# Gates and ups with both halves of h in one 512-column product, added at the evacuation

## The reference, cut to what matters

```python
proj = jnp.einsum("bsd,dn->bsn", h, w_in)
q, k, v, f_logit, g_b, g_c, hc, gate_conv, gate_attn = jnp.split(proj, _SPLITS, axis=-1)
...
merged = jax.nn.sigmoid(gate_conv) * ya_d + jax.nn.sigmoid(gate_attn) * yb_d
...
gu = jnp.einsum("bsd,df->bsf", h, w_gate_up)
g, u = jnp.split(gu, 2, axis=-1)
return jnp.einsum("bsf,fd->bsd", jax.nn.silu(g) * u, w_down)
```

## Time and profile before

| | |
|---|---|
| median of 3 runs | 1022.47 us |
| the profiled execution | 1022.51 us |
| its span, first to last instruction | 1021.0 us |
| time around the span | 1.5 us |
| instructions | 16052 |
| mean granted TensorE clock | 0.995 |
| HBM read | 223.54 MB |

### The profile page before, as it was taken

The page is one execution under the profiler, slowest core; times in us unless marked ns, Lnnn a source line. Parts: engine busy times, 40 slices in busy tenths (PEclk is TensorE's granted clock), DMA queues, the critical chain, the costliest instruction groups (busy, mean ns, idle before and its releaser), DMA issues.

```text
span 1021.0 us, 16052 instructions
## 1 busy us (share of the span) xinstructions
PE 995.3 (97%) x6874; PEld 914.1 (90%) x6874; DVE 688.0 (67%) x986; ACT 491.4 (48%) x688; POOL 33.3 (3%) x51
## 2 busy tenths in 40 slices
PE   7999999899999999999999999999999899999997
PEld 6988899789898998899889999997997689999996
DVE  5766756769757768887778768667676766545443
ACT  5644544454334345555564334455667664434341
POOL 3000000010000000100000000001000010000000
PEclk9999999999999999999999999999999999999999
DMA  9663367556897775786467778875643257555511
GB/s 366 262 229 101 126 251 280 206 188 246 314 259 289 296 278 193 265 313 247 166 248 266 300 280 308 312 293 179 214 137 125 83 130 262 171 201 171 201 42 41
DMA packets 33303, 225.65 MB, mean 221 GB/s; under 512 B 3997, under 2 KB 4277, under 8 KB 6864
## 3 DMA queue, kind: packets, MB, share of 16 engines
q1 hardware_dynamic: 31104, 219.00, 59.8%
q0 software_dynamic: 1552, 4.88, 1.4%
q10 hardware_dynamic: 576, 0.74, 0.2%
HBM read 223.54 MB, written 1.08 MB: 220 GB/s over the span
## 4 chain that ended last, share of the span: by engine, by line
PE 88%; DVE 6%; ACT 3%; issue 1%; DMA 1%; POOL 0%; ACTq 0%; DVEq 0%
PE psum L569 18%; PE psum L571 18%; PE psum L570 18%; PE psum L595 8%; PE psum L596 8%; PE psum L597 8%; DVE low L496 2%; PE psum L814 2%; ACT high L490 1%; PE psum L659 1%; PE psum L660 1%; PE psum L661 1%; PE psum L311 1%; PE psum L880 1%; DMA x_res<-in_x 1%
## 5 line engine op out<-in xcount | busy, mean ns | idle before, releaser
L496 DVE TENSOR_TENSOR low<-raw,high 128x2048 fp32r<-128x2048 f32 (+1 forms) x160 | 362.3, 2276 | 162.7 <-ACT high L490 162.1
L569 PE MATMUL psum<-h_hi,high 128*128 128x256 f32 x1504 | 428.6, 285 | 0.0
L571 PE MATMUL psum<-h_hi,low 128*128 128x256 f32 x1504 | 425.5, 283 | 0.0
L570 PE MATMUL psum<-h_lo,high 128*128 128x256 f32 x1504 | 425.5, 283 | 0.0
L490 ACT ACTIVATE high<-raw 128x2048 fp32r<-128x2048 f32 (+1 forms) x160 | 301.0, 1899 | 53.1 <-DMA raw<-in_gate_up 27.9
L569 PEld LDWEIGHTS psum<-h_hi,high 128*128 128x128 f32 x1504 | 288.4, 192 | 5.2 <-issue 2.3
L570 PEld LDWEIGHTS psum<-h_lo,high 128*128 128x128 f32 x1504 | 288.5, 192 | 1.1
L571 PEld LDWEIGHTS psum<-h_hi,low 128*128 128x128 f32 x1504 | 288.5, 192 | 0.0
L595 PE MATMUL psum<-high,y_hi 128*128 128x512 f32 x328 | 129.1, 394 | 2.9 <-DVE y_lo L902 1.7
L596 PE MATMUL psum<-low,y_hi 128*128 128x512 f32 x328 | 128.0, 390 | 0.0
L597 PE MATMUL psum<-high,y_lo 128*128 128x512 f32 x328 | 127.7, 389 | 0.0
(11 more groups left out here) (173 smaller groups left out, 904.7 us busy)
## 6 DMA issues: line engine op xcount, KB each, us to landing
raw<-in_gate_up SPq DMA_DIRECT2D x66, 1024.0 KB, 5.1
raw<-in_ada SPq DMA_DIRECT2D x48, 1024.0 KB, 6.4
raw<-in_down SPq DMA_DIRECT2D x33, 1024.0 KB, 5.3
raw<-in_mix SPq DMA_DIRECT2D x14, 1024.0 KB, 5.1
raw<-in_moba_qk SPq DMA_DIRECT2D x8, 1024.0 KB, 7.2
raw<-in_diff_qk SPq DMA_DIRECT2D x8, 1024.0 KB, 6.2
raw<-in_qk SPq DMA_DIRECT2D x4, 1024.0 KB, 14.7
raw<-in_branch SPq DMA_DIRECT2D x4, 1024.0 KB, 6.1
```

The lines of the kernel that those rows point to most:

```text
L496: nc.vector.tensor_tensor(low[i % N_RAW][:, s], raw[i % N_RAW][:, s], high[n % N_HI][:, s].bitcast(F32), ALU.subtract).then_inc(*rest.up(key))
L569: nc.tensor.matmul(to, a, hi(k), start=first, stop=False)
L570: nc.tensor.matmul(to, a, lo(k), start=False, stop=False)
L571: m = nc.tensor.matmul(to, r, hi(k), start=False, stop=last and j > j0)
```

## The change

h_hi and h_lo become the two halves of one tile, so that for a given k they lie side by side as 512 columns. A new `pe_both` takes the place of `pe_still` for the eight mixer gates and for gates and ups of groups 1 to 10 of each feed-forward part (68 slabs: 8 and 60). For each k and column block it issues two matmuls in place of three: the weights' high half with both halves of h (512 columns), and the weights' low half with h_hi (256 columns, onto the first 256). A column block now fills a whole bank, so a product takes two neighbouring banks, the first of them even. The sum over the two halves is made at the evacuation: ACT copies the second halves to SBUF (`act_low`), DVE adds the first halves out of PSUM (`dve_low`, in place), and only then come Silu or Sigmoid (ACT, now from SBUF) and gate times up (DVE, now from SBUF). A product's banks are free when `dve_low` has run (`joined`). The transposes of probabilities 6 and 7 in the first attention get banks 4 and 5 by number.

```diff
--- before.py
+++ after.py
@@ -177,8 +177,8 @@
         low = [sb(f"low{i}", [P, SLAB], F32R) for i in range(N_RAW)]
         high = [sb(f"high{i}", [P, SLAB], F32R) for i in range(N_HI)]
         x_res = sb("x_res", [P, NT, D])
-        h_hi = sb("h_hi", [P, KC, S], F32R)
-        h_lo = sb("h_lo", [P, KC, S], F32R)
+        h_both = sb("h_both", [P, KC, 2, S], F32R)
+        h_hi, h_lo = h_both[:, :, 0, :], h_both[:, :, 1, :]
         y_hi = sb("y_hi", [P, KC, S], F32R)
         y_lo = sb("y_lo", [P, KC, S], F32R)
         work = sb("work", [P, 2 * NT * D])
@@ -209,7 +209,8 @@
         ident_r = sb("ident_r", [H, H], F32R)
         diff_stat = sb("diff_stat", [P, NT * H])
         minus_half = sb("minus_half", [P, NT * H])
-        psum = [ctx.enter_context(nc.psum_tensor(f"psum{i}", [P, 512], F32)) for i in range(8)]
+        psum_two = [ctx.enter_context(nc.psum_tensor(f"psum{i}", [P, 2, 512], F32)) for i in range(4)]
+        psum = [psum_two[i // 2][:, i % 2, :] for i in range(8)]
         gain_dram = nc.dram_tensor("gain_dram", (4, D), F32, kind="Internal").ap()
         bias_dram = nc.dram_tensor("bias_dram", (H, BIAS_W), F32, kind="Internal").ap()
 
@@ -285,6 +286,29 @@
             owner[at] = list(freed)
             bank_of[key] = at
             return psum[at]
+
+        def two_banks(key, *freed):
+
+            turn[0] += turn[0] % 2
+            yield from bank(key, *freed)
+            yield from bank((key, "second"), *freed)
+            return psum_two[bank_of[key] // 2]
+
+        def halves(key):
+
+            o = psum_two[bank_of[key] // 2]
+            return o[:, :, 0:S], o[:, :, S:2 * S]
+
+        def act_low(key, place, *free):
+
+            yield from act.wait_ge(slab, key)
+            for signal, done in free:
+                yield from act.wait_ge(signal, done)
+            nc.scalar.activation(place, halves(key)[1], ACT.Copy).then_inc(*evacuated.up(("low", *key)))
+
+        def dve_low(key, place):
+            yield from dve.wait_ge(evacuated, ("low", *key))
+            nc.vector.tensor_tensor(place, halves(key)[0], place, ALU.add).then_inc(*joined.up(key))
 
 
         def columns_of(stage):
@@ -569,6 +593,22 @@
                         nc.tensor.matmul(to, a, hi(k), start=first, stop=False)
                         nc.tensor.matmul(to, a, lo(k), start=False, stop=False)
                         m = nc.tensor.matmul(to, r, hi(k), start=False, stop=last and j > j0)
+            m.then_inc(*slab.up(n, (name, index), *alias))
+
+        def pe_both(name, index, ready, freed, alias=()):
+
+            n = NUM[name, index]
+            yield from pe.wait_ge(rest, n)
+            wh = high[n % N_HI][:, :].rearrange("p (k n) -> p k n", k=KC)
+            wl = low[SLOT[n]][:, :].rearrange("p (k n) -> p k n", k=KC)
+            o = yield from two_banks((name, index), freed)
+            for k in range(KC):
+                for signal, key in ready(k):
+                    yield from pe.wait_ge(signal, key)
+                for j in range(2):
+                    a, r = wh[:, k, j * P:(j + 1) * P], wl[:, k, j * P:(j + 1) * P]
+                    nc.tensor.matmul(o[:, j, :], a, h_both[:, k, :, :], start=k == 0, stop=False)
+                    m = nc.tensor.matmul(o[:, j, 0:S], r, h_hi[:, k, :], start=False, stop=k == KC - 1)
             m.then_inc(*slab.up(n, (name, index), *alias))
 
         def pe_moving(name, parts, data, ready, kcs, k_all, freed, tag, between={}):
@@ -695,11 +735,11 @@
             yield from pe_turn(before, 1)
             yield from pe_rows(f, 1)
             for g in range(1, FG):
-                yield from pe_still(gate_up, base * 2 * FG + g, h_of, h_ready(before), [[(evacuated, ("silu", f, g))]])
+                yield from pe_both(gate_up, base * 2 * FG + g, h_ready(before), (joined, (gate_up, base * 2 * FG + g)))
                 if g == 1:
                     yield from pe_turn_rows(f)
-                yield from pe_still(gate_up, base * 2 * FG + FG + g, h_of, h_ready(before), [[(produced, ("hidden", f, g))]],
-                                    [("up", f)] if g == FG - 1 else [])
+                yield from pe_both(gate_up, base * 2 * FG + FG + g, h_ready(before), (joined, (gate_up, base * 2 * FG + FG + g)),
+                                   [("up", f)] if g == FG - 1 else [])
                 if g < FG - 2:
                     yield from pe_down(f, g - 1)
                 if g in meanwhile:
@@ -715,11 +755,13 @@
             for g in range(1, FG):
                 gate, up = (gate_up, base * 2 * FG + g), (gate_up, base * 2 * FG + FG + g)
                 yield from act_next(*gate)
-                yield from act.wait_ge(slab, gate)
-                nc.scalar.activation(ffn_tmp(g)[:, 0], pair(bank_of[*gate, 0]), ACT.Silu).then_inc(*evacuated.up(("silu", f, g)))
+                yield from act_low(gate, ffn_tmp(g)[:, 0])
+                yield from act.wait_ge(joined, gate)
+                nc.scalar.activation(ffn_tmp(g)[:, 0], ffn_tmp(g)[:, 0], ACT.Silu).then_inc(*evacuated.up(("silu", f, g)))
                 if g == 1:
                     yield from act_turn_rows(f)
                 yield from act_next(*up, AHEAD if g < FG - 1 else FAR)
+                yield from act_low(up, ffn_tmp(g)[:, 1])
                 yield from act.wait_ge(produced, ("hidden", f, g))
                 if g >= 4:
                     yield from act.wait_ge(slab, NUM[down, base * FG + g - 4])
@@ -737,12 +779,14 @@
             for g in range(1, FG):
                 gate, up = (gate_up, base * 2 * FG + g), (gate_up, base * 2 * FG + FG + g)
                 yield from dve_next(*gate)
+                yield from dve_low(gate, ffn_tmp(g)[:, 0])
                 if g == 1:
                     yield from dve_turn_rows(f)
                 yield from dve_next(*up, AHEAD if g < FG - 1 else FAR)
+                yield from dve_low(up, ffn_tmp(g)[:, 1])
                 yield from dve.wait_ge(evacuated, ("silu", f, g))
-                yield from dve.wait_ge(slab, up)
-                nc.vector.tensor_tensor(ffn_tmp(g)[:, 1], pair(bank_of[*up, 0]), ffn_tmp(g)[:, 0], ALU.mult).then_inc(
+                yield from dve.wait_ge(joined, up)
+                nc.vector.tensor_tensor(ffn_tmp(g)[:, 1], ffn_tmp(g)[:, 1], ffn_tmp(g)[:, 0], ALU.mult).then_inc(
                     *produced.up(("hidden", f, g)))
                 yield from dve.wait_ge(hi_made, ("hidden", f, g))
                 s = slice(2 * (g % 4), 2 * (g % 4) + 2)
@@ -872,9 +916,9 @@
                                                    op0=ALU.mult, op1=ALU.add)
             m.then_inc(*weighted.up((tag, h)))
 
-        def pe_turn_probs(tag, h):
+        def pe_turn_probs(tag, h, at=None):
             z = prob[probs_of(tag, h)[0]]
-            o = yield from bank(("turn", tag, h), (probs_copied, (tag, h)))
+            o = yield from bank(("turn", tag, h), (probs_copied, (tag, h)), at=at)
             yield from pe.wait_ge(weighted, (tag, h))
             for c in range(3):
                 m = nc.tensor.transpose(o[:, c * P:(c + 1) * P], z[:, c * P:(c + 1) * P], ident)
@@ -919,7 +963,7 @@
                 nc.tensor.matmul(o[rows, 0:S], v(0), p[:, 0:S], start=True, stop=False)
                 nc.tensor.matmul(o[rows, P:S], v(1), p[:, S:3 * P], start=False, stop=True).then_inc(*applied.up(("s1", h)))
             if 0 <= n - 2 < H:
-                yield from pe_turn_probs("s1", n - 2)
+                yield from pe_turn_probs("s1", n - 2, n - 4 if n >= H else None)
             if n < H:
                 h = n
                 part = slice((h % 2) * HD1, (h % 2 + 1) * HD1)
@@ -1130,7 +1174,7 @@
                 yield from pe_attend1(6 + g)
             for n in range(2):
                 for g in range(4):
-                    yield from pe_still("mix", 6 + 4 * n + g, h_of, ready, [[(evacuated, ("gate", n, g))]])
+                    yield from pe_both("mix", 6 + 4 * n + g, ready, (joined, ("mix", 6 + 4 * n + g)))
                     if n == 0 and g < 3:
                         yield from pe_attend1(H + g)
             conv_of = (lambda k: y_hi[:, AC + k, :], lambda k: y_lo[:, AC + k, :])
@@ -1257,10 +1301,11 @@
                 for g in range(4):
                     index = 6 + 4 * n + g
                     yield from act_next("mix", index)
-                    yield from act.wait_ge(slab, ("mix", index))
+                    two = slice(2 * g, 2 * g + 2)
                     yield from act.wait_ge(lo_made, ("conv", 1))
-                    nc.scalar.activation(place[:, 2 * g:2 * g + 2, :], pair(bank_of["mix", index, 0]), ACT.Sigmoid).then_inc(
-                        *evacuated.up(("gate", n, g)))
+                    yield from act_low(("mix", index), place[:, two, :])
+                    yield from act.wait_ge(joined, ("mix", index))
+                    nc.scalar.activation(place[:, two, :], place[:, two, :], ACT.Sigmoid).then_inc(*evacuated.up(("gate", n, g)))
                     if n == 0 and g < 3:
```

(6 more changed lines are left out.)

## The result

The changed kernel takes 1042.03 us (median of 4 runs, 1038.28 to 1043.22), the kernel before 1023.19 us in the same comparison (1021.98 to 1024.10). The ratio is 1.0175, 95% interval 1.0156 to 1.0193: slower by 19 us. The profiled execution took 1043.22 us with a span of 1041.7 us, 20.7 us more than the span before. The direction was forecast, the size was not: 1031.4 us was predicted, and 1042 lies above the range of 1016 to 1039.

The account below looks back on a forecast made before the run. The prediction took PE, busy 97% of the span, as the bound. From 1022.5 us it took 11.8 saved, 17.3 lost to waits and 3.4 to the clock, giving 1031.4 us, range 1016 to 1039.

Parts of the forecast that it names:

- saving of the pairs: PE matmuls of all 68 slabs: two matmuls per set instead of three save 11.9 ns a set, 12.9 us in all.
- the six slabs ahead of a wait: Gate 1 three times, up 5, up 10 twice: their saving is void, 1.1 us, leaving 11.8 saved.
- up 1 waits for gate 1's banks: Up 1 in feed-forward parts 0, 1, 2 waits for DVE's addition: 3.8, 5.1 and 1.5 us, together 10.4.
- gate 6 waits for the flips' copies: Part 0: four flip products take banks 0 to 3, so gate 6 waits for DVE's copies, 3.4 us late.
- down 10 waits for the last y_lo: Ends of parts 0 and 1: the last hidden group's added copy and additions delay down 10 by 1.4 and 2.1 us.
- the clock: PE's granted clock falls behind two of five new gaps: 3.4 us, between 0 for none and 8.6 for all.
- (a): Rival at up 1 and the flips: additions come early, up 1 waits about 1 us, 1016.5 us; chance 0.11.
- (d): Rival: DVE's loop becomes the bound where ada slabs are dense, 9 us more, 1040 us; chance 0.08.
- (b): Rival: up 1's stalls let other engines get ahead; flips and ends cost nothing, clock stays; 1021.1 us; chance 0.11.
- (c): Rival on PE's pairs: no fixed cost goes away, 2.5 ns saved a set instead of 11.9; 1041.6 us; chance 0.05.

Follow-up runs that it names:

- the first experiment: Changed kernel with the transposes of group 0 given bank 4 by number; 1028.58 us against 1024.49 for the kernel before, ratio 1.0040.
- The filled wait: Changed kernel with 17, 23 and 6 small unused fp32 matmuls on PE ahead of up 1; 1036.05 us against 1024.49 for the kernel before.
- the grouped form: Changed kernel with all 16 matmuls of 512 columns issued before the 16 of 256 in each product; 1035.80 us, kernel before 1024.49.
- the version with the other two edits: Changed kernel with bank 4 for group 0's transposes, flips two at a time and widths grouped; 1019.04 us, kernel before 1022.58.
- y_lo behind the addition: Changed kernel, DVE making gate 1's addition ahead of the rests for group 1; 1038.74 us against 1022.58 for the kernel before.
- the norm behind the put-off rests: Changed kernel with bank 4 for transposes, split flips and 3 slabs rounded ahead for group 10 instead of 5; 1025.33 us, kernel before 1023.71.

## Why the prediction was wrong

Term by term, in us, from the starts of the same products in the two profiled executions:

| term | predicted | measured |
|---|---|---|
| saving of the pairs, without the six slabs ahead of a wait (992 pairs of 6.9 ns) | -11.8 | -6.8 |
| up 1 waits for gate 1's banks | +10.4 | +10.6 |
| gate 6 waits for the flips' copies | +3.4 | +3.9 |
| down 10 waits for the last y_lo | +3.5 | +4.4 |
| the clock | +3.4 | +8.2 |
| start of the kernel (first gate of the mixer 113.31 against 112.55) | 0 | +0.8 |
| sum | +8.9 | +21.1, of 20.7 in the spans |

The mechanism was right: slower by waits that the bank rotation and DVE's order make, at the places named. Up 1's waits came within 0.5 us of the sizes read off DVE's rows and went away with a change of a single bank; flips and ends came out 0.5 and 0.9 us longer than forecast. The start of the kernel is not the change's: in the first experiment, with the same pairs, the first gate is at 112.43. Two terms of the sum were mis-sized, by about 5 us each: the clock and the pair.

**The clock.** "Between none falling (0) and all five (8.6 us) I take two: 3.4 us". All five fell in the profiled execution. Against the same product at full clock, up 1 took 7.20 us in part 0 and 7.83 in part 1 in place of 5.72 (part 2), gate 6 and up 6 together 12.73 in place of 11.17 (the first experiment's, below), and from down 10 to the next layer's first query product it was 26.3 us twice in place of 24.8: 1.5 + 2.1 + 1.6 + 1.5 + 1.5 = 8.2. So the price of a fall was right (8.6 for five), and the count of two was not.

```profile
316.83 0.47 PE L610 MATMUL psum<-h_both,high 128*128 128x512 f32 x1 [2.43 <-DVE bias L835]
...
328.00 0.39 PE L635 MATMUL psum<-high,y_hi 128*128 128x512 f32 x1
```

The count had two faults. The prediction called a fall beyond 3 us likely, had three such gaps (5, 4 and 3.4 us), and still took two falls in all. And it set the window 794 to 798 of the earlier trace rows, with a fall, against 810 to 814, without one, as nearly the same idle time; the trace has waits of 2.48 and 1.67 us there. By the counts of all runs above, the three long waits were near certain to bring a fall. That both ends, with 2.85 and 2.77 us, did so too is in part chance: waits of that length went without it in other executions. The filled wait shows that it is idle time that brings the fall. As far as the runs tell, the falls also set where an execution of the changed kernel lands: the one of 1038.28 us had a mean clock of 0.989, the three others 0.985 or 0.986.

**The pair.** "I take 11.9 because it comes from the same type, weights of the same size and the same engine state". The type and size were the same, the order of issue was not: both paces had been read from streams of one width, and in the alternating order most pairs take 352.8 ns in place of 347.8. A single step at a resolution of 10 ns, 333.18 to 333.41 of the earlier trace rows, could not show 5 ns, and 992 pairs make 5 us of them. Why most products lose them and up 3 and up 6 don't is not known. The bound from below was there (nothing saved), and the truth lies a little over half of the way from it to 11.9. The Trainium skill's "TensorE: Matmul & The Clock Gate", section Back-to-back issue gap, would by its formula N/2.4 + 2.5 make the saving 2.5 ns for a set. Neither the pairs (6.9) nor the grouped form (359.7 - 347.2 = 12.5, with 11.11 us for 32 sets) agree.

The flips' term was low by 0.5 since ACT's copy of gate 5 stood behind a rounding that waited 1.7 us for a transfer. In the ends' term down 10 of part 1 waited 2.77 us in place of 2.1, and that of part 0 2.85, 1.7 more than the 1.17 us before the change, in place of 1.4.

Of the rivals, (a) and (d) did not occur: the additions came where DVE's order puts them, and no group from 2 to 9 shows a wait for a rest. (b) had the waits at flips and ends gone and the clock kept, and they were all there. Of (c), a saving of 2.5 ns a set, half was true (6.9); that its 1041.6 us is the measured time to 0.4 us is chance, since it holds no more falls of the clock than the forecast. The range of 1016 to 1039 holds either of the two errors alone, 1036.6 us with all five clocks falling or 1036.4 with pairs of 6.9 ns, but not both together, which give 1041.6.

## What to carry to other kernels

Before banks or buffers are made larger, write out the rotation by hand over every place where something is put between two products: a tile that takes two of four slots can make each odd guest a full wait, and giving the guest a slot of its own cost nothing here. Charge the waits that are well beyond one after which the trace shows a lower clock with the clock's price as well, in full, and the ones about as long with a share of it: here that was 8 us on top of 19. And when instructions of two widths replace a uniform stream, time them grouped by width too.

## What the runs showed that was not expected

- The order of issue matters on PE: the same 32 matmuls of 512 and 256 moving columns take 5.65 us alternating in most products and 5.55 us grouped. Over 68 products grouping was worth 0.67% of the kernel, and 0.7% in the version with the other two edits. Two alternating products ran at 5.55 us as well, so it is not the change of width alone.
- The price of a bank depends on what DVE has waiting. In part 2, with no ada slabs, the same conflict cost 1.5 us; in part 1, with two of them among the rests, 5.2.
- Taking away a wait uncovered another on the same engine (y_lo behind the addition; the norm behind the put-off rests): 3 us gained of 11 in the one case, nothing in the other.
- The same wait of 2.4 to 3.2 us brought a fall of the clock in some executions and not in others, so the time of a kernel with such waits can vary from run to run.
- The granted clock rose again by itself after each fall, and a filler of small matmuls during the wait kept it at 1.00.
